# The low halves of the streamed weights made on GpSimd instead of VectorE, in a two-model transformer kernel on one core

## The reference, cut to what matters

```python
for li in range(DEPTH):                       # first block
    h = h + mixer(rms_norm(h, norm_mix_g[li]), w_in[li], w_branch[li], w_out[li], ...)
    h = h + conv_ffn(rms_norm(h, norm_ffn_g[li]), w_ffn_in[li], conv_w[li], conv_b[li], w_ffn_out[li], valid)
...
for l in range(DEPTH):                        # second block
    h = rmsnorm(x, attn_norm_g[l])
    ... = jnp.split(h @ w_in[l], split_points, axis=-1)
    merged = gates[:, :, 0, :] * (branches[0] @ w_branch[l, 0]) + ...
    x = x + merged @ w_out[l]
    h2 = rmsnorm(x, ffn_norm_g[l])
    x = x + (jax.nn.silu(h2 @ w_ffn_gate[l]) * (h2 @ w_ffn_up[l])) @ w_ffn_down[l]
```

## Time and profile before

| | |
|---|---|
| median of 3 runs | 2705.21 us (2704.2 to 2705.54) |
| profiled execution, its own time | 2708.24 us |
| profiled execution, its span | 2706.5 us |
| mean granted TensorE clock | 0.954 |
| TensorE busy | 2538.7 us (94%) |
| VectorE busy | 1898.1 us (70%) |
| ScalarE busy | 1356.2 us (50%) |
| GpSimd busy | 0.2 us |
| weights read | 684 slabs of 512 KB, mean 136 GB/s |

### The profile page before, as it was taken

One profiled execution on the slowest core, in us unless ns is written; L12 is line 12 of the kernel. 1 busy time (PEld: TensorE's weight loads), 2 busy tenths in 40 slices (PEclk: granted clock), 3 DMA queues, 4 the chain that ended last, 5 costly groups with the idle time before them and its releaser, 6 DMA issues.

```text
span 2706.5 us, 50167 instructions
## 1 busy us (share of the span) xinstructions
PE 2538.7 (94%) x19014; PEld 2414.9 (89%) x19014; DVE 1898.1 (70%) x3587; ACT 1356.2 (50%) x2232; POOL 0.2 (0%) x4
## 2 busy tenths in 40 slices
PE   7999998998999999998999998999999989999998
PEld 7999997798999998997788998888989989889998
DVE  5698756767875689856677875676766556667674
ACT  5554555655544644555655544453544454445443
POOL 0000000000000000000000000000000000000000
PEclk9999998899999999998899998888999997889999
DMA  5433332244444433342234444332445543334554
GB/s 207 150 116 102 119 132 93 80 148 140 158 165 157 162 109 102 114 144 86 94 129 145 161 165 134 118 109 94 156 157 185 184 146 103 109 101 157 172 184 136
DMA packets 100431, 366.75 MB, mean 136 GB/s; under 512 B 11633, under 2 KB 12145, under 8 KB 99825
## 3 DMA queue, kind: packets, MB, share of 16 engines
q1 hardware_dynamic: 100208, 363.69, 40.5%
HBM read 362.60 MB, written 1.05 MB: 134 GB/s over the span
## 4 chain that ended last, share of the span: by engine, by line
PE 59%; DVE 23%; DVEq 6%; ACT 4%; issue 4%; ACTq 2%; DMA 1%; SPq 0%
PE psum L440 59%; DVE ring_lo L1272 7%; ACT arena L852 2%; DVE arena L1484 2%; ACT ring_hi L865 1%; DMA ring<-w 1%; DVEq L1483 1%; DVE arena_r L1262 1%; DVE arena L1303 1%; DVE arena L1311 1%; DVE arena_r L1260 1%; ACTq L994 1%; DVE arena L1660 1%; DVE arena L1662 1%; DVEq L1254 1%
## 5 line engine op out<-in xcount | busy, mean ns | idle before, releaser
L440 PE MATMUL psum<-hn_hi,ring_hi 128*128 128x272 f32 (+1 forms) x3920 | 1178.5, 302 | 58.2 <-DVE ring_lo L1272 35.3
L440 PE MATMUL psum<-hn_hi,ring_lo 128*128 128x272 f32 (+1 forms) x3920 | 1149.3, 294 | 0.0
L440 PE MATMUL psum<-hn_lo,ring_hi 128*128 128x272 f32 (+1 forms) x3920 | 1110.5, 291 | 0.0
L1272 DVE TENSOR_TENSOR ring_lo<-ring,ring_hi 128x1024 fp32r<-128x1024 f32 x684 | 830.3, 1224 | 277.6 <-ACT ring_hi L865 228.5
L440 PEld LDWEIGHTS psum<-hn_hi,ring_hi 128*128 128x128 f32 x3920 | 775.2, 198 | 90.6 <-issue 69.5
L865 ACT ACTIVATE ring_hi<-ring 128x1024 fp32r<-128x1024 f32 x684 | 714.9, 1055 | 219.6 <-DMA ring<-w 188.3
L440 PEld LDWEIGHTS psum<-hn_hi,ring_lo 128*128 128x128 f32 x3920 | 774.7, 198 | 0.0
L440 PEld LDWEIGHTS psum<-hn_lo,ring_hi 128*128 128x128 f32 x3920 | 753.1, 195 | 1.6
L852 ACT ACTIVATE arena<-psum 128x272 f32<-128x272 f32 (+5 forms) x720 | 251.8, 366 | 748.5 <-PE psum L440 640.3
L440 PE MATMUL psum<-arena_r,ring_hi 128*128 128x272 f32 (+1 forms) x2996 | 562.7, 287 | 15.5 <-DVEq L1254 11.0
L440 PEld LDWEIGHTS psum<-arena_r,ring_hi 128*128 128x128 f32 x2996 | 468.9, 189 | 19.6 <-DVEq L1254 12.5
(11 more groups left out here) (151 smaller groups left out, 1489.0 us busy)
## 6 DMA issues: line engine op xcount, KB each, us to landing
ring<-w SPq DMA_DIRECT2D x684, 512.0 KB, 3.3
cst<-consts SPq DMA_DIRECT2D x1, 2120.0 KB, 14.7
x_sb<-x_meta SPq DMA_DIRECT2D x1, 1088.0 KB, 4.9
out<-x_sb SPq DMA_DIRECT2D x1, 1024.0 KB, 3.9
arena<-lam SPq DMA_DIRECT2D x1, 256.0 KB, 4.2
par_sb<-par SPq DMA_DIRECT2D x1, 193.0 KB, 4.7
pos_sb<-positions SPq DMA_DIRECT2D x1, 128.0 KB, 6.5
cst<-consts SPq DMA_DIRECT2D x1, 65.5 KB, 4.9
```

The lines of the kernel that those rows point to most:

```text
L440: i = nc.tensor.matmul(out_, lhsT=lhsT, rhs=rhs, start=first, stop=last)
L1272: V.tensor_tensor(ring_lo[:, slot], ring[:, slot], ring_hi[:, slot].bitcast(F32), ALU.subtract)\
```

## The change

GpSimd gets a program of its own. For each slab it waits for the high half, makes the low half in four instructions of 128x256 in the same place, and signals `slab_lo` with the last of them. VectorE's `low_slab` still counts the slabs, but returns before its wait and its instruction for every slab in `POOL_SLABS`, which are all of them.

```diff
+POOL_SLABS = range(SLABS)
...
                 k = lows["fed"]
                 lows["fed"] = k + 1
+                if k in POOL_SLABS:
+                    return
                 slot = slice((k % RING) * SLAB * P, (k % RING + 1) * SLAB * P)
                 dve.wait_ge(slab_hi[k % RING], k // RING + 1)
                 V.tensor_tensor(ring_lo[:, slot], ring[:, slot], ring_hi[:, slot].bitcast(F32), ALU.subtract)\
...
+        @block.gpsimd
+        def _(pool):
+
+            for k in sorted(POOL_SLABS):
+                pool.wait_ge(slab_hi[k % RING], k // RING + 1)
+                for q in range(4):
+                    part = slice((k % RING) * SLAB * P + q * 2 * P, (k % RING) * SLAB * P + (q + 1) * 2 * P)
+                    i = nc.gpsimd.tensor_tensor(ring_lo[:, part], ring[:, part], ring_hi[:, part].bitcast(F32), ALU.subtract)
+                i.then_inc(slab_lo[k % RING], 1)
```

## The result

The changed kernel takes 2766.19 us (median of 4 runs, 2764.02 to 2770.03) against 2705.38 us: ratio 1.0228, 95% interval 1.0216 to 1.0241. It is 61 us slower. The forecast was 2810 us, slower, so the direction held and the size was 105 us where 61 came.

What follows compares the result with a forecast made beforehand. VectorE was taken to bound the heads and first up-projection, TensorE the second block's feed-forward. Terms 61 + 24 + 22 + 18 - 20 = +105 us on 2708.2 gave 2813, less 3: 2810 us; range 2640 to 2980.

Steps and rivals of the forecast that it cites:

- The bound of each stage: VectorE sets the pace in gated heads and first block's up-projection (by 0.6 us a pair), TensorE in second block's feed-forward.
- The price of a quarter: One GpSimd instruction of 128x256, a quarter of a slab, costs 692 ns, one pass for each input; 2.77 us a slab.
- Turns: GpSimd and VectorE alternate strictly for VectorE's instructions with two SBUF inputs and its casts; likeliest case, 2740 to 2900 us.
- The rival of a slow GpSimd: A quarter takes 0.8 us or more, over both feed-forwards' cadence: 3000 to about 3300 us; chance of slower than 2900: 0.22.
- that of cheap quarters: Engines take turns but a quarter costs only 0.56 us: about even, 2695 to 2720 us; chance 0.13.
- The rival of undisturbed engines: VectorE and GpSimd run side by side; heads and first block's up-projection fall to TensorE's pace: about 2640 us; chance 0.23.
- Step 1: Gated heads: each grows from 25.2 to 29 us, the middle between full and no hiding; +61 us (0 to +123).
- Step 2: First block's up-projection: 5.54 us of quarters plus 1.63 of shared VectorE instructions, 7.17 against 6.62 a pair; +24 us.
- Step 3: Second block's up-projection: a pair of tiles takes 6.26 us against 5.76; +22 us.
- Step 4: First block's last merge branch, second block's output projections and merges go over TensorE's time; ring absorbs half: +18 us.
- Step 5: Attention stages rid of VectorE's slabs and TensorE's waits shrinking, against later first slabs behind layer norms: -20 us.

Runs made afterwards that it cites:

- experiment 2: The changed kernel, but VectorE makes the 80 slabs of the gated heads and GpSimd the other 604: 2714.07 us.
- experiment 3: The changed kernel with no low halves made by either engine; TensorE takes the high half in place of the low one: 2583.99 us.
- experiment 10: The kernel of experiment 4, with every second slab of the gated heads on GpSimd too: 2680.07 us.
- experiment 1: The changed kernel with a drain of GpSimd behind the four quarters of each slab: 2789.99 us.
- experiment 9: The changed kernel with a drain of GpSimd behind every second slab only: 2748.79 us.
- experiment 4: The changed kernel, but GpSimd makes only the 136 slabs of the first block's differential attention and up-projection, VectorE all others: 2657.37 us.
- experiment 8: The kernel of experiment 4, with every second slab of the four projection stages on GpSimd too: 2664.33 us.
- experiment 5: The changed kernel with one GpSimd instruction of 128x1024 a slab in place of four of 128x256: 2990.59 us.
- experiment 6: The changed kernel with eight GpSimd instructions of 128x128 a slab in place of four of 128x256: 2946.73 us.

## Why the prediction was right, and where its sum was off

**The bound of each stage** held: heads and the first up-projection by VectorE, the second feed-forward by TensorE. That VectorE binds the heads is shown by experiment 2, and by the 27.9 us a head (223.3 / 8) with GpSimd in place of 24.2, and experiment 3 shows TensorE's pace behind: 186.5 us for the heads' stage. (The one head of the earlier trace rows, 25.2 us, is longer than the mean.)

**The price of a quarter** held. I took 692 ns, one pass for each input; back to back it is 696 ns. With 2,341 ns of pitch at 1024 columns (its lowest tenth) and 418 at 128, it is 2.15 ns a column and about 0.14 us fixed; 256 columns give 0.69 us by that. "One pass for each input" was a guess from VectorE's rows that hit. The rival of a slow GpSimd falls with it, and so does that of cheap quarters. The Trainium skill (GPSIMD Engine Reference, 3.1) has 2.6 cycles an element, by its 1.2 GHz an estimate of 2.17 ns: the slope agrees, and the fixed part is what an estimate by proportion leaves out.

**Turns** held in kind: 443 to 726 ns for two SBUF inputs, 499 unchanged for PSUM, 443 again beside memsets. The Trainium skill (SBUF, State Buffer, Who interferes with whom) states that a VectorE instruction with two SBUF inputs contends with a GpSimd instruction that reads SBUF, and not with one that only writes; the trace agrees. That the later of the two is blocked until the other's one instruction ends does not cover the ten long waits, which lasted over many. The rival of undisturbed engines is refuted by the same rows. I had counted VectorE's multiplications of one SBUF input by a scalar as free of turns; they are not (348 to 654 ns).

**Step 1, the heads:** +61 us forecast, +58.8 measured. The middle between no hiding and full hiding was a guess that hit, and by luck: its 19.1 us is the head's length less the slabs (25.2 - 6.1), but VectorE's busy time less the slabs is 16.75 us, and with that the same middle gives 27.8 us, +42 us. The fall of the clock from 1.00 to 0.93, in no term, came on top. Experiments 2 and 10 show that it is GpSimd's share that costs.

**Step 2, the first block's up-projection, failed: +24 us forecast, -15 measured.** I had charged each shared instruction of VectorE to GpSimd in full, 1.63 us on top of 5.54, for 7.17 us a pair. The stage takes 141.4 / 22 = 6.43. The timeline has 16 quarters in 12.49 us there:

```profile
703.58 12.49 POOL L1939 TENSOR_TENSOR ring_lo<-ring,ring_hi 128x256 fp32r<-128x256 f32 x16
```

That is 0.78 us a quarter, 6.2 a pair, where 0.696 is the pace alone. Four shared instructions a pair cost GpSimd 8 x 0.085 = 0.7 us, not 1.63: some 0.17 us each. The rest of an instruction's length overlaps with the other engine's. So GpSimd did not lose the whole length of a shared instruction, which "held exclusively" in the prediction would mean; the measurement decides. VectorE, which had bound, was rid of 2.45 us of slabs a pair, and its new waits are shorter than that. The bound moved from VectorE at 6.62 us to GpSimd at 6.2 to 6.4, a gain.

**Step 3, the second block's up-projection:** +22 forecast, +5.7 measured, the same term too large. GpSimd did become the bound, at 2.91 us a slab and not 3.13. Of a slab's cost only 0.03 us over the 2.88 of before is left, some 1.5 us a layer; most of the rest of the first layer's +4.3 us lies in its first eight slabs.

**Step 4, other full stretches:** +18 forecast; all stages that the table does not name, +10.8.

**Step 5, the gains where there is room:** -20 forecast, -31.2 in the differential attention alone. I took them from TensorE's waits and the share of the low halves in the chain. What was freed is VectorE's queue between short dependent steps: ScalarE's wait for it fell from 37.3 us (420 to 560 us before) to 17.8 us (460 to 580 us after). The clock rose in the same stage (0.88 to 0.95), which the forecast had nowhere.

**What no step had:** VectorE held off for a whole run of GpSimd instructions, 31 us in the projections (+8.2, +8.6, +4.9, +9.9). Experiments 1 and 9 take these waits away with nothing but a gap, and the loss goes with them (+31.6 to +8.0 and +2.1). I had each wait end with the quarter in progress. Without this loss the changed kernel would be at about 2735 us (an estimate, 2766 - 32), so two errors of opposite sign made the forecast look nearer than its working was: the turns charged too much in steps 2 and 3 by 56 us, the long waits were missing with 32.

What stays open: how the hold comes about. In the changed kernel it hit instructions that arrived after 14 or more quarters in a row that neither a wait for a high half nor a turn of VectorE had interrupted, and none of those that arrived earlier; at up to eight in a row (experiment 9) it never came. In experiments 4, 8 and 10 GpSimd worked through up to 144 or 160 quarters with its waits met, but VectorE interrupted it after nine at most, and it never came either. In experiment 2 one came after a run that I count as 10. With whole slabs (experiment 5) it never came, but runs were short there. With eighths (experiment 6), of the delayed instructions that arrived after 11 to 14 in a row 19 were held and 29 were not, so the number alone does not decide; a time does not fit better (11 eighths are 4.6 us, 11 quarters 7.7 us). What ends a hold without a gap is open too.

## What to carry to other kernels

An idle engine that reads SBUF is not free beside VectorE: count, stage by stage, VectorE's instructions with two SBUF inputs, its casts and its operations of one SBUF input with a scalar that lie in the way, and give the idle engine work only where they do not set the pace. Here all slabs on GpSimd cost 61 us, and a fifth of them, chosen by measuring each stage in both traces, gained 48. If an engine works through a long queue whose waits are all met, look at the longest instruction of its neighbour, not the mean, and try a gap in the queue, as seldom as will do: behind every second slab it gained 17 us here, behind every slab it lost 24. And read a stage's granted clock before its busy times: waits that a change makes or takes away can move it.

## What was not expected of the hardware

- One VectorE instruction of 0.35 us lasted 31.3 us, until GpSimd's run of 58 instructions ended, and its twin 28.3 us, ended by no gap; with a gap behind each eighth instruction the longest was 1.2 us.
- A drain on GpSimd costs 0.18 us of idle time; turns cost GpSimd 0.17 us for each shared instruction of VectorE, and VectorE 0.28 us on average (443 to 726 ns).
- Of three sizes of GpSimd's instructions the middle one is best here: 128 columns 2946.7 us, 256 columns 2766.2, 1024 columns 2990.6.
- Memsets on GpSimd leave two-input instructions alone (443 ns) and lengthen casts at 256 columns (294 to 625 ns).
- In the differential attention the same matmuls kept TensorE busy for 118.1 us in place of 128.5, at a granted clock of 0.95 in place of 0.88.
